# The differential attention of a two-part network on one core: projections dealt over a head's four steps, PSUM banks assigned by use, and one maximum over both score halves

## The chip, the cores and the metric

The kernel runs on one core of a Trainium2 chip. The metric is the device time of one execution in microseconds (us), median of the runs. An execution taken with the hardware profiler gives the trace. The engines are PE (TensorE, the matrix engine), DVE (VectorE), ACT (ScalarE), POOL (GpSimd) and SP (SyncE, which issues the DMA transfers).

## The reference

A first block (two layers: FFN, mixer, FFN) and a second block (two layers of another kind) run one after the other on 512 tokens of width 1024. The change lies in the mixer of the first layer, a differential attention with 8 heads, 512 queries (tokens x) and 768 keys (256 of a context y and the 512 tokens):

```python
def diff_attn_core(q, k, v, lam):
    s = jnp.einsum('bqhcd,bkhcd->bhcqk', q.astype(jnp.float32), k.astype(jnp.float32))
    p = jax.nn.softmax(s * (1.0 / math.sqrt(HEAD_DIM)), axis=-1)
    a = p[:, :, 0] - lam * p[:, :, 1]
    return jnp.einsum('bhqk,bkhe->bqhe', a.astype(v.dtype), v)
```

Each head has two halves c of 64 dimensions. q and k are normalised per half (RMS), q and the token part of k are rotated (RoPE), and v has 128 dimensions. The head's output is normalised (RMS over 128), and `w_o` maps all heads back to 1024. `lam` is a scalar from four learned vectors. Everything is float32.

## The kernel before

**Arithmetic.** Each float32 operand of a large product is split into a high part (fp32r) and the low remainder, and a product is three matmuls: high x high, high x low, low x high. ACT casts the high part (`ACT.Copy` into an R tensor), DVE subtracts to get the low part. Weights come from HBM in blocks of eight 128x128 tiles, in the order of use; ACT (L845) and DVE (L1319) split each block, four split blocks are held, and a block may be split once PE has released the one four before it (`stream(upto[...])` on ACT and DVE stands in their programs at the place where that is done).

**Order.** Five engine programs are written out by hand; each engine works its list in order, and every step waits on named steps of others. Layout is features on partitions, tokens along the free axis.

**Attention.** Head h is worked in four steps qt of 128 queries; n = 4h + qt counts to 32. In step n PE writes the scores of both halves (`scores`, 128 x 768 each, K = 64: half 0 on rows 0 to 63 of the array, half 1 on rows 64 to 127). DVE takes the maximum of each half (L1560) and scales it (L1563), ACT takes the two exponentials with row sums (L1012), and DVE combines both halves into one matrix (L1532 to L1538, `combine`). In step n+1 PE transposes that matrix (`turn`, "pt", L394), ACT (L985) and DVE (L1515) split it, and every second step PE multiplies the values with it (`values`, 18 matmuls of 256 columns). Between these stands the preparation of the next head H = h + 1, which `piece` deals out: q is projected in step 0 (24 matmuls of 512 columns), its sums of squares and its rotation (a permutation matmul) come in step 1 together with the projection of k (8 x 3 x (512 + 256) columns), the rotation of k, the projection of v and the spread of k's scales in step 2, and the transposition of v in step 3. Head h - 1's output is normalised in step 2. In the last head the output projections `wo` of heads 0 to 5 take the place of the preparation, two tiles per step, and the parts of heads 6 and 7 follow at the end.

**PSUM.** Banks 0 to 5 form a ring: `take` gives the next one or two, whatever the use, and waits until the last user has freed them. The head's output (PG, bank 6) and the sums (PN, bank 7) have banks of their own.

```python
        def take(name, n):
            nonlocal pos
            n = 2 if n > 512 else 1
            pos += -pos % n
            i = pos % 6
            pos += n
```

**lam.** It is computed by DVE at the start of attention, with an exponential of ACT (whose table load, L994, takes place there).

## Time and profile before

| what | value |
|---|---|
| runs | 3828.03, 3831.35, 3834.58 us; median 3831.35 |
| profiled execution | 3833.75 us, its span 3832.0 us, mean granted PE clock 0.948 of full |
| PE busy | 3579.2 us (93% of the span) |
| DVE, ACT, POOL busy | 1932.7, 1272.9, 350.1 us |
| chain that ended last | PE 85%, DVE 9%, ACT 3%, POOL 1% |
| attention with the norms before and after (649.7 to 1215.0 us) | 565.3 us, PE busy 488.5, DVE 306.2, ACT 210.3, clock 0.84 |

The granted clock has two levels, 2.4 GHz (1.0) and 1.2 GHz (0.5); the clock of a stretch is the mean over it. Times in rows are from the start of the span. A matmul's record is longer than its distance to the next one, since they are pipelined; distances of starts tell what one costs in a run of them. "[1.63 <-DVE QKV L1510]" behind a row is idle time of that engine before it and what ended it.

### The profile page before, as it was taken

What the parts mean: (1) busy time and instruction counts of PE and PEld (TensorE: products, weight loads), DVE (VectorE), ACT (ScalarE), POOL (GpSimd) and SP (SyncE); (2) the same over time, 40 slices, a digit from 0 to 9 for tenths busy, and PEclk for the clock granted to TensorE, in tenths of its full rate; (3) what the DMA queues carried; (4) which work ended last, traced back from release to release, by engine and by line L of the source; (5) the groups of instructions that cost most, each with busy time, mean ns of one, the idle gap of its engine ahead of it and who ended that gap; (6) DMA issues with size and microseconds to landing.
All of it is one profiled execution on the core that took longest, in us unless ns stands there. A gap on an engine that the chain in (4) does not pass through costs nothing.

```text
span 3832.0 us, 40505 instructions
## 1 busy us (share of the span) xinstructions
PE 3579.2 (93%) x17064; PEld 2949.4 (77%) x17064; DVE 1932.7 (50%) x2742; ACT 1272.9 (33%) x1771; POOL 350.1 (9%) x200
## 2 busy tenths in 40 slices
PE   2999998899998999899999999989999999999998
PEld 2888887677776888788877888766788877678887
DVE  8434334455555544454444333386564647656464
ACT  4322123333333322322333323333442433344242
POOL 3301001000101000000000000330100023010001
PEclk9999998888888999999999999998899999899999
DMA  5323232000002545354322222220122222012221
GB/s 194 135 84 127 89 116 72 33 28 28 28 34 91 185 147 170 118 173 154 116 77 81 96 99 94 85 79 6 51 98 99 95 77 84 6 50 88 99 94 60
DMA packets 95654, 348.83 MB, mean 91 GB/s; under 512 B 10608, under 2 KB 10864, under 8 KB 94960
## 3 DMA queue, kind: packets, MB, share of 16 engines
q1 hardware_dynamic: 94176, 343.06, 26.2%
q10 hardware_dynamic: 1296, 3.18, 0.2%
q8 instruction: 134, 2.20, 0.2%
q14 instruction: 48, 0.39, 0.0%
HBM read 344.10 MB, written 2.10 MB: 90 GB/s over the span
## 4 chain that ended last, share of the span: by engine, by line
PE 85%; DVE 9%; ACT 3%; POOL 1%; issue 1%; DMA 0%; ACTq 0%; SPq 0%; DVEq 0%; POOLq 0%
PE PS L325 84%; DVE CAC L1689 2%; DVE WL L1319 1%; PE PS L394 1%; DVE ST L1560 1%; ACT WH L845 1%; DVE SCR L1346 1%; POOL SM L1974 1%; ACT G L1012 0%; DVE X L1661 0%; ACT HH L896 0%; DVE ST L1780 0%; ACT G L884 0%; DVE X L1670 0%; POOL PTF L1967 0%
## 5 line engine op out<-in xcount | busy, mean ns | idle before, releaser
L325 PE MATMUL PS<-HH,WH 128*128 128x512 f32 (+1 forms) x3120 | 1204.5, 386 | 58.3 <-DVE HL L1676 18.1
L1319 DVE TENSOR_TENSOR WL<-RAW,WH 128x1024 fp32r<-128x1024 f32 x462 | 576.7, 1249 | 1261.5 <-ACT WH L845 1261.4
L325 PE MATMUL PS<-HL,WH 128*128 128x512 f32 (+1 forms) x3120 | 1187.8, 381 | 0.0
L325 PE MATMUL PS<-HH,WL 128*128 128x512 f32 (+1 forms) x3120 | 1183.1, 379 | 0.0
L845 ACT ACTIVATE WH<-RAW 128x1024 fp32r<-128x1024 f32 x496 | 524.4, 1057 | 1472.7 <-PE PS L325 1460.4
L325 PEld LDWEIGHTS PS<-HH,WH 128*128 128x128 f32 x3120 | 603.0, 193 | 183.7 <-DVE HL L1421 19.4
L325 PEld LDWEIGHTS PS<-HL,WH 128*128 128x128 f32 x3120 | 602.5, 193 | 113.7 <-issue 7.0
L325 PEld LDWEIGHTS PS<-HH,WL 128*128 128x128 f32 x3120 | 599.8, 192 | 111.1
L325 PE MATMUL PS<-AH,WH 128*128 128x512 f32 x1392 | 525.2, 377 | 0.0
L325 PE MATMUL PS<-AL,WH 128*128 128x512 f32 x1392 | 524.8, 377 | 0.0
L325 PE MATMUL PS<-AH,WL 128*128 128x512 f32 x1392 | 523.5, 376 | 0.0
L325 PEld LDWEIGHTS PS<-AH,WH 128*128 128x128 f32 x1392 | 262.5, 189 | 49.0 <-issue 0.3
L325 PEld LDWEIGHTS PS<-AH,WL 128*128 128x128 f32 x1392 | 261.8, 188 | 48.5
L325 PEld LDWEIGHTS PS<-AL,WH 128*128 128x128 f32 x1392 | 262.3, 188 | 47.6
L1346 DVE CUSTOM_DVE_ANT_0 RAW<-RAW,PTF 128x1024 f32<-128x1024 f32 x128 | 154.0, 1236 | 26.4 <-POOL PTF L1967 26.4
L2010 POOL TENSOR_TENSOR ACC<-ACC,X 128x512 f32<-128x512 f32 x25 | 32.3, 1292 | 1270.6 <-DVE X L1908 692.0
L1987 POOL TENSOR_TENSOR ACC<-ACC,G 128x512 f32<-128x512 f32 (+1 forms) x30 | 42.8, 1428 | 1131.7 <-ACT G L869 831.0
L919 ACT ACTIVATE AH<-G 128x512 fp32r<-128x512 f32 (+1 forms) x88 | 60.4, 686 | 210.1 <-DVE G L1435 210.1
L1974 POOL TENSOR_TENSOR SM<-SM,MH 128x4 f32<-128x4 f32 (+3 forms) x42 | 70.1, 1671 | 595.4 <-DVE SM L1379 595.2
L1689 DVE SCALAR_TENSOR_TENSOR CAC<-CIN,VB,CAC 128x512 f32<-128x512 f32 x120 | 109.2, 955 | 0.9
L1438 DVE TENSOR_TENSOR AL<-G,AH 128x512 fp32r<-128x512 f32 (+1 forms) x88 | 69.4, 789 | 66.2 <-ACT AH L919 66.2
L1967 POOL TENSOR_TENSOR PTF<-RAW,PTF 128x1024 f32<-128x1024 f32 x28 | 79.3, 2830 | 220.8 <-ACT PTF L853 116.1
(266 smaller groups left out, 3321.5 us busy)
## 6 DMA issues: line engine op xcount, KB each, us to landing
RAW<-wst SPq DMA_DIRECT2D x640, 512.0 KB, 3.3
X<-xT SPq DMA_DIRECT2D x1, 2048.0 KB, 12.3
out<-X SPq DMA_DIRECT2D x8, 256.0 KB, 2.0
PTF<-cb SPq DMA_DIRECT2D x1, 1024.0 KB, 4.9
Y<-yT SPq DMA_DIRECT2D x1, 1024.0 KB, 6.3
PTF<-cb ACTq DMA_DIRECT2D x1, 1024.0 KB, 4.8
HM<-sg ACTq DMA_DIRECT2D x4, 256.0 KB, 3.6
ROPE<-rope SPq DMA_DIRECT2D x1, 512.0 KB, 4.2
```

Of the source, the lines that this page charges most:

```text
L325: return e.matmul(o, l, r, start=start, stop=stop)
L394: m = e.transpose(bk[:, t * 128:(t + 1) * 128], src[:, t * 128:(t + 1) * 128], ident)
L845: e.activation(split_block(b)[0], raw_block(s), ACT.Copy).then_inc(*did("act_done", ("whi", b)))
L919: e.activation(aview(f - f0, N)[0], s, ACT.Copy).then_inc(*did("act_done", ("ahi", st, f)))
L1319: e.tensor_tensor(lo, raw_block(s), f32(hi), ALU.subtract).then_inc(*did("dve_done", ("wlo", b)))
L1346: e.tensor_tensor_reduce(dst, raw, CB[:, 0:1024], 1.0, 0.0, ALU.mult, ALU.add, mcol(l, ch, k, 0)).then_inc(*did("dve_done", ("gx", l, j)))
L1438: e.tensor_tensor(lo, s, f32(hi), ALU.subtract).then_inc(*did("dve_done", ("a", st, f), ("gdone", use)))
L1560: e.tensor_reduce(s8[:, c:c + 1], bank["s", n, c][:, 0:768], AXX, ALU.max).then_inc(*did("dve_done", ("max", n, c)))
L1689: e.scalar_tensor_tensor(out=CA[i], in0=AP[i][:, k:k + 512], scalar=v2(f"caw{l}", i * 31 + k), in1=CA[i], op0=ALU.mult, op1=ALU.add).then_ ...
L1967: e.tensor_tensor((PROD, SCR[3])[p], raw_block(s), CB[:, 1024:2048], ALU.mult).then_inc(*did("pool_done", ("gprod", l, j)))
L1974: e.tensor_tensor(sm(name, b, n), sm(name, a, n), MH[:, 0:n], ALU.pow).then_inc(*did("pool_done", ("rs", name)))
L1987: e.tensor_tensor(ACC[:, 0:N], ACC[:, 0:N], G(use, N), ALU.add).then_inc(*did("pool_done", ("acc", up, m), ("gdone", use)))
```

## The change

Nothing is computed otherwise; order, buffers and banks change, only in the attention and in the place of `lam`.

- **Projections over all four steps.** Step 0: k of head H (with the transposition of head h's v between its halves, in `between`). Step 1: sums of k's squares, q (k's permutation in the middle). Step 2: sums of q's squares, the last 256 columns of v ("v2", q's permutation in the middle), the spread of k's scales, the sums for head h - 1's output. Step 3: the spread for that output, the first 512 columns of v. ACT evicts each at the start of the next step, ahead of the softmax. k and q no longer share scratch buffers (KS_, KSQ, QS, QSQ, `vs(h)`).
- **PSUM by use** (`hold`). Banks 0 to 2: scores. 3 and 4: transposed probabilities, transposed v, spread of k. 5 (and 6 for k): projections. 6: sums, permutations, spread of o. 7: head outputs. The other stages still use `take`.
- **Scores.** Both halves lie in 1536 contiguous columns of three banks. The matmuls alternate between the halves; a wait of PE on its own "s bank 1" keeps the two halves from writing bank 1 at once. One reduction takes both maxima and one operation scales both; both exponentials wait for it, and both halves are freed by the second.
- **Last head and tail.** `wo` tiles 2, 2, 2, 1 per step and one after the last transposition, all in bank 5; then six tiles together for heads 6 and 7, head 7's sums and spread between their first and second K tile, two more tiles singly.
- **Start.** Head 0 is projected k, q, v2, v one after another, and k of head 1 before the first scores.
- **lam** is worked out before the first norm, from a small tensor with a DMA of its own.

PE's program, cut to its core (`key_stat` and `key_permute` have sisters for q, `key_spread`, `out_stat` and `out_spread` for the rest, of the same form):

```diff
+        def hold(name, n, i, frees=None):
+            n = 2 if n > 512 else 1
+            prior = [u for u in users[i:i + n] if u is not None]
+            users[i:i + n] = [frees or ("free", name)] * n
+            bank[name] = PS[:, i * 512:(i + n) * 512]
+            return bank[name], prior
...
             i = pos % 6
             pos += n
-            prior = [u for u in users[i:i + n] if u is not None]
-            users[i:i + n] = [name] * n
-            bank[name] = PS[:, i * 512:(i + n) * 512]
-            return bank[name], prior
+            return hold(name, 512 * n, i)
         def allowed():
             nonlocal ptr
...
+            def project(name, us, c0, c1, into, final=True, between=None):
+                nonlocal released
+                bk, prior = hold(name, c1 - c0, into)
+                q.wait_ge("wlo", us[0][2])
+                for p in prior:
+                    q.wait_ge(*p)
+                for k, (hi, lo, step, _) in enumerate(xs):
+                    q.wait_ge(*step)
+                    if k == 4 and between:
+                        between()
+                    for c in range(c0, c1, 512):
+                        d = min(c + 512, c1)
+                        o = bk[:, c - c0:d - c0]
+                        mm(o, us[k][0], hi[:, c:d], k == 0, False)
+                        mm(o, us[k][0], lo[:, c:d], False, False)
+                        m = mm(o, us[k][1], hi[:, c:d], False, k == 7)
+                steps = [("tile", name)]
+                if final:
+                    steps.append(("wfree", us[0][2]))
+                    released += 1
+                m.then_inc(*did("pe_done", *steps))
+                upto[name] = allowed()
...
+            def key_stat(h):
+                stat(("k", h), [(KSQ, 128, bd, ("ksq", h))], 6, 2, into=6)
+            def key_permute(h):
+                permute(("pk", h), permA, KS_[:, 0:512], ("ks", h), into=6)
...
+            def turn_values(h):
+                bk, prior = hold(("vt", h), 768, 3)
+                a, b = vs(h)
+                for p in prior:
+                    q.wait_ge(*p)
+                q.wait_ge("vs", h)
+                for t in range(4):
+                    e.transpose(bk[:, t * 128:(t + 1) * 128], a[:, t * 128:(t + 1) * 128], ident)
+                q.wait_ge("vs2", h)
+                for t in range(2):
+                    m = e.transpose(bk[:, 512 + t * 128:640 + t * 128], b[:, t * 128:(t + 1) * 128], ident)
+                m.then_inc(*did("pe_done", ("tile", ("vt", h))))
...
             def scores(n):
                 h, qt = n // 4, n % 4
-                for c in range(2):
-                    bk, prior = take(("s", n, c), NT)
-                    rows = slice(c * 64, c * 64 + 64)
...
+                _, prior = hold(("s", n), 768, 0)
+                _, more = hold(("s", n), 512, 2)
+                o = bank["s", n] = PS[:, 0:1536]
+                q.wait_ge("qsplit", h)
+                q.wait_ge("ksplit", h)
+                for p in prior + more:
+                    q.wait_ge(*p)
+                Q = [[a[c * 64:c * 64 + 64, qt * 128:qt * 128 + 128] for a in QKV[h % 2]] for c in range(2)]
+                K = [[a[c * 64:c * 64 + 64, 512:1280] for a in QKV[h % 2]] for c in range(2)]
+                for i, (a, b) in enumerate(((0, 0), (0, 1), (1, 0))):
+                    m = mm(o[:, 512:768], Q[0][a], K[0][b][:, 512:768], i == 0, i == 2)
+                    if i == 2:
+                        m.then_inc(*did("pe_done", ("s bank 1", n)))
+                    mm(o[:, 1024:1536], Q[1][a], K[1][b][:, 256:768], i == 0, i == 2)
+                for i, (a, b) in enumerate(((0, 0), (0, 1), (1, 0))):
+                    m = mm(o[:, 0:512], Q[0][a], K[0][b][:, 0:512], i == 0, i == 2)
+                    if i == 2:
+                        m.then_inc(*did("pe_done", ("s first", n)))
+                    q.wait_ge("s bank 1", n)
+                    m = mm(o[:, 768:1024], Q[1][a], K[1][b][:, 0:256], i == 0, i == 2)
+                m.then_inc(*did("pe_done", ("tile", ("s", n))))
...
+            project(("k", 0), weights(1024, 0), 0, NT, 5)
+            project(("q", 0), weights(0, 0), 0, NX, 0)
+            key_stat(0)
+            v = weights(2048, 0)
+            project(("v2", 0), v, NX, NT, 3, False, lambda: key_permute(0))
+            project(("v", 0), v, 0, NX, 4)
+            query_stat(0)
+            query_permute(0, 0)
+            key_spread(0, 1)
             for n in range(32):
-                h, qt = n // 4, n % 4
+                h, qt, H = n // 4, n % 4, n // 4 + 1
+                if n == 0:
+                    project(("k", 1), weights(1024, 1), 0, NT, 5, True, lambda: turn_values(0))
                 scores(n)
-                if qt == 2 and h:
-                    stat(("o", h - 1), [(OSQ, 128, ones, ("osq", h - 1))], 4, 1)
                 if n >= 3 and n % 2:
                     values((n - 2) // 4, (n - 2) % 4 // 2)
                 if n:
-                    turn(("pt", n - 1), G(("p", n - 1, 0)), 6, ("pc", n - 1), ("gdone", ("p", n - 1, 0)))
-                if h < 7:
-                    piece(h + 1, qt)
+                    turn_p(n - 1)
+                if H < 8:
+                    if qt == 0 and n:
+                        project(("k", H), weights(1024, H), 0, NT, 5, True, lambda: turn_values(h))
+                    if qt == 1:
+                        key_stat(H)
+                        project(("q", H), weights(0, H), 0, NX, 5, True, lambda: key_permute(H))
+                    if qt == 2:
+                        query_stat(H)
+                        v = weights(2048, H)
+                        project(("v2", H), v, NX, NT, 5, False, lambda: query_permute(H, 6))
+                        key_spread(H, 3)
+                        if h:
+                            out_stat(h - 1)
+                        if H == 7:
+                            project(("v", H), v, 0, NX, 5)
+                    if qt == 3:
+                        if h:
+                            out_spread(h - 1)
+                        if H < 7:
+                            project(("v", H), v, 0, NX, 5)
                 else:
-                    for m in (2 * qt, 2 * qt + 1):
-                        lin([output(m, 0, 6)], oxs(0, 6))
-                if qt == 2 and h:
-                    spread(("o", h - 1), 4, None, ("rs", ("o", h - 1)))
-            turn(("pt", 31), G(("p", 31, 0)), 6, ("pc", 31), ("gdone", ("p", 31, 0)))
+                    if qt == 0:
+                        turn_values(7)
+                    if qt == 2:
...
+                    for m in ((0, 1), (2, 3), (4, 5), (6,))[qt]:
+                        lin([output(m, 0, 6)], oxs(0, 6), [5])
+                        if m == 4:
+                            out_spread(6)
+            turn_p(31)
...
+            lin([output(7, 0, 6)], oxs(0, 6), [5])
             values(7, 1)
-            stat(("o", 7), [(OSQ, 128, ones, ("osq", 7))], 4, 1)
-            spread(("o", 7), 4, None, ("rs", ("o", 7)), ("attention done",))
-            lin([output(m, 6, 8) for m in range(4)], oxs(6, 8))
-            for m in range(4, 8):
-                lin([output(m, 6, 8)], oxs(6, 8))
+            def last():
+                out_stat(7)
+                out_spread(7, ("attention done",))
+            lin([output(m, 6, 8) for m in range(6)], oxs(6, 8), [0, 1, 2, 3, 4, 5], {1: last})
+            for m in (6, 7):
+                lin([output(m, 6, 8)], oxs(6, 8), [m - 6])
```

ACT's program, in part:

```diff
+            def softmax(n):
+                h, qt = n // 4, n % 4
+                s8 = st8(n)
+                for c in range(2):
+                    use = ("p", n, c)
+                    q.wait_ge("gdone", GBEFORE[use])
+                    q.wait_ge("negmax", n)
+                    steps = [("exp", n, c)]
+                    if c:
...
-                h, qt = n // 4, n % 4
-                for c in range(2):
-                    s8, use = st8(n), ("p", n, c)
-                    q.wait_ge("gdone", GBEFORE[use])
-                    q.wait_ge("negmax", n, c)
-                    steps = [("exp", n, c), ("free", ("s", n, c))]
-                    if qt == 3 and c == 1:
-                        steps.append(("smfree", ("q", h)))
-                    e.activation(G(use), bank["s", n, c][:, 0:768], ACT.Exp, bias=s8[:, 2 + c:3 + c],
-                                 scale=sm(("q", h), 24 + qt * 2 + c, 1), accum_out=s8[:, 4 + c:5 + c]).then_inc(*did("act_done", *steps))
+                h, qt, H = n // 4, n % 4, n // 4 + 1
+                if qt == 0 and n:
+                    v_evict(h)
+                if H < 8:
+                    if qt == 1:
+                        k_evict(H)
+                    if qt == 2:
+                        q_evict(H)
+                    if qt == 3:
```

DVE's and SP's programs, in part:

```diff
-            e.tensor_tensor(LMS[:, 64:128], lamv[:, 128:192], lamv[:, 192:256], ALU.mult).then_inc(*did("dve_done", ("lam1",)))
+            q.wait_ge("lam in")
+            e.tensor_tensor(LMS[:, 0:64], LAMV[:, 0:64], LAMV[:, 64:128], ALU.mult).then_inc(*did("dve_done", ("lam0",)))
...
+            def row_max(n):
+                s8, r = st8(n), sm(("q", n // 4), 24 + n % 4 * 2, 2)
+                q.wait_ge("tile", ("s", n))
+                e.tensor_reduce(s8[:, 0:2], bank["s", n].rearrange("p (c k) -> p c k", c=2), AXX, ALU.max).then_inc(*did("dve_done", ("max", n)))
+                q.wait_ge("max", n)
+                q.wait_ge("qscale", n // 4)
+                e.scalar_tensor_tensor(out=s8[:, 2:4], in0=s8[:, 0:2], scalar=-1.0, in1=r, op0=ALU.mult, op1=ALU.mult).then_inc(*did("dve_done", ("negmax", n)))
...
-                    stat(("o", h - 1), 1, 4, 1.0 / 128, 1e-6)
+                h, qt, H = n // 4, n % 4, n // 4 + 1
+                row_max(n)
+                if H < 8 and qt == 1:
+                    stat(("k", H), 1, 12, 1.0 / 64, 1e-6)
+                if H < 8 and qt == 2:
+                    stat(("q", H), 1, 8, 1.0 / 64, 1e-6)
                 if n:
                     p_split(n - 1)
                 combine(n)
-                if h < 7:
-                    if qt == 0 and h:
-                        stream(upto["q", h + 1])
+                if H < 8:
+                    if qt == 0 and n:
+                        v_split(h)
+                        stream(upto["v", h])
                     if qt == 1:
-                        q_rotate(h + 1)
-                        stream(upto["k", h + 1])
+                        k_rotate(H)
+                        stream(upto["k", H])
                     if qt == 2:
-                        k_rotate(h + 1)
-                        stream(upto["v", h + 1])
...
+                e.dma_start(LAMV[:, :], vec1[:, V1["lam"][0]:NV1]).then_inc(*did("lam_in", ("lam in",), by=16))
```

## Rows read from the trace of the kernel before

**Rows 1.** The page: the chain that ended last, by engine.
```profile
PE 85%; DVE 9%; ACT 3%; POOL 1%; issue 1%; DMA 0%; ACTq 0%; SPq 0%; DVEq 0%; POOLq 0%
```
**Rows 2.** Windows: us, busy (count) of PE, PEld, DVE, ACT, POOL; clock, DMA share, GB/s.
```profile
656.60:720.40 63.80, 45.02 (x187) 36.25 (x187) 25.33 (x41) 25.51 (x36) 4.28 (x2) 0.76 0.10 34
720.40:768.10 47.70, 43.44 (x232) 35.53 (x233) 28.14 (x50) 17.24 (x27) 4.67 (x2) 0.84 0.07 22
...
1112.90:1198.40 85.50, 73.85 (x344) 61.13 (x344) 44.10 (x67) 25.52 (x39) 4.61 (x4) 0.83 0.15 50
768.10:1112.90 344.80, 317.95 (x1721) 261.67 (x1720) 197.58 (x336) 129.94 (x204) 34.01 (x18) 0.88 0.08 28
```
**Rows 3.** Waits of PE, 649 to 1225 us: total, times, longest.
```profile
PE PS L325 <- ACT G L1012: 10.1, 15, 2.4
```
**Rows 4.** Timeline of DVE in one step of the steady part.
```profile
883.08 0.95 DVE L1560 TENSOR_REDUCE ST<-PS 128x1 f32<-128x768 f32 x1
...
885.18 0.21 DVE L1563 TENSOR_SCALAR ST<-ST,SM 128x1 f32<-128x1 f32 x1
887.24 0.96 DVE L1515 TENSOR_TENSOR PTL<-PS,PTH 128x768 fp32r<-128x768 f32 x1 [1.85 <-ACT PTH L985]
...
889.15 1.02 DVE L1538 SCALAR_TENSOR_TENSOR G<-G,ST 128x768 f32<-128x768 f32 x1
```
**Rows 5.** Timeline of ACT in the same step.
```profile
884.31 0.99 ACT L1012 ACTIVATE G<-PS,ST,SM 128x768 f32<-128x768 f32 x1 [4.28 <-DVE ST L1563]
...
886.41 0.80 ACT L985 ACTIVATE PTH<-PS 128x768 fp32r<-128x768 f32 x1
```
**Rows 6.** Timeline of PE: end of k's projection, scores, sums, transposition.
```profile
906.52 0.40 PE L325 MATMUL PS<-HH,WH 128*128 128x512 f32 x1
...
907.22 0.28 PE L325 MATMUL PS<-HH,WH 128*128 128x256 f32 x1
907.34 0.28 PE L325 MATMUL PS<-HL,WH 128*128 128x256 f32 x1
...
907.66 0.62 PE L325 MATMUL PS<-QKV 64*128 64x512 f32 x2
908.13 0.39 PE L325 MATMUL PS<-QKV,QKV 64*128 64x512 f32 x1
...
909.37 1.05 PE L325 MATMUL PS<-CST,Y 128*128 128x1 f32 x8
910.43 0.87 PE L394 MATMUL PS<-CST,G 128*128 128x128 f32 x6
```
**Rows 7.** Timeline of PE, a permutation.
```profile
898.24 1.10 PE L325 MATMUL PS<-Y,CST 128*128 128x512 f32 x2
```
**Rows 8.** Groups of DVE and POOL, 720 to 1170 us: count, busy, mean ns, idle.
```profile
L1319 DVE TENSOR_TENSOR WL<-RAW,WH 128x1024 fp32r<-128x1024 f32 x25 | 30.6, 1225 | 93.0 <-ACT WH L845 92.9
...
L1386 DVE TENSOR_TENSOR Y<-PS,ROPE 128x512 f32<-128x512 f32 x14 | 9.6, 682 | 0.0
...
L1974 POOL TENSOR_TENSOR SM<-SM,MH 128x4 f32<-128x4 f32 x7 | 7.0, 1006 | 96.9 <-DVE SM L1379 96.9
```
**Rows 9.** Timeline of PE behind the gap at a head's last step.
```profile
883.31 1.51 PE L394 MATMUL PS<-CST,G 128*128 128x128 f32 x6 [1.63 <-DVE QKV L1510]
```
**Rows 10.** Windows: the same place, columns as in rows 2.
```profile
882.20:889.00 6.80, 5.07 (x14) 3.98 (x15) 4.81 (x10) 2.87 (x5) 0.00 (x0) 0.50 0.00 0
```
**Rows 11.** Timeline of PE in the tail: output projection of heads 6, 7.
```profile
1185.33 0.80 PE L325 MATMUL PS<-HH,WH 128*128 128x512 f32 x1 [1.45 <-DVE HL L1527]
```
**Rows 12.** Timeline of DVE in the start of attention: last normed tile, lam.
```profile
670.07 0.96 DVE L1421 TENSOR_TENSOR HL<-G,HH 128x768 fp32r<-128x768 f32 x1 [1.12 <-ACT HH L896]
...
690.73 0.22 DVE L1465 TENSOR_TENSOR LMS<-VA 128x64 f32<-128x64 f32 x1
...
691.33 0.14 DVE L1469 TENSOR_SCALAR SGV<-VA 128x1 f32<-128x1 f32 x1
```
**Rows 13.** Timeline of PE: the first scores.
```profile
720.36 0.58 PE L325 MATMUL PS<-QKV 64*128 64x512 f32 x2 [2.50 <-DVE QKV L1510]
```

More of the change, by code:

```diff
@@ L1364, in stat @@
         def stat(name, nsrc, n, inv, eps):
-            sums = PN[:, 0:n]
+            region = bank["st", name]
+            sums = region[:, 0:n]
             q.wait_ge("stat", name)
@@ L1919, in _ @@
         stream(upto["start"])
+        lam()
         norm("f00")
```

346 lines of the change are left out of this document (175 added, 171 removed).

## Prediction

> **What bounds the kernel now.** I read the page first: PE carries 85% of the chain that ended last [rows 1], so time is won only where PE works, waits, or runs at the low clock. Then windows by stage: the change touches the 541.8 us from 656.6 to 1198.4. In it lie the start up to the first scores (63.8 us), head 0 (47.7), the stretch from head 0's end to head 7 (344.8, six heads, 57.5 each) and head 7 with the tail (85.5) [rows 2]. In the six heads the clock means 0.88: with the two levels 2.4 and 1.2 GHz that is 24% of the time, 13.8 us a head, at 1.2 GHz.
>
> Next, what PE's work costs at 2.4 GHz, by distances of starts: three matmuls of 512 columns take 907.22 - 906.52 = 0.70 us, one of 256 0.12 us, so a K tile of 768 columns takes 1.05, k's or v's projection 8.3 and q's 5.6 us. A set of scores takes 909.37 - 907.66 = 1.71 us, a transposition 0.87, sums 0.13 per matmul (1.05 for eight) [rows 6], a permutation 1.1 [rows 7]. Values are 18 x 0.12 = 2.2 us a pair. One head: projections 22.2, scores 6.8, values 4.4, transpositions 5 x 0.7 = 3.5 (they overlap their neighbours a little), 28 sums and 20 spread matmuls 6, permutations 2.2, together 45. The other 12.5 us of a head are idle and low clock. Waits that the list names are small, the largest 10.1 us for exponentials in all of attention [rows 3], and the gap at a head's last step, where no projection lies, is 1.6 us before a transposition that then runs at half speed (1.51 us, against 0.87) [rows 6, 9]; the 6.8 us from 882.2 on all lie at 1.2 GHz [rows 10]. So what is to be had is the idle time, and more than it the low clock behind it.
>
> **The change, part by part.** The count of projections, values, transpositions and sums stays.
>
> Scores: the rows of before already show the two halves overlapping. Twelve matmuls in sequence would be 6 x 0.23 + 6 x 0.12 = 2.1 us, and they took 1.71 [rows 6]. Alternated, each half needs 1.05, and the wait on bank 1 sits in the middle; the bounds are 1.05 and 2.1, and I take 1.4, nearer to 1.05 than 1.71 is, with one restart in it. That saves 0.3 a step. The Trainium skill (TensorEngine Tiling (Array Packing), Theoretical Speedup) gives up to twofold for a contraction of 64; by it 2.1 would become 1.05 and 32 sets would save 21 us rather than my 10 against 1.71. The overlap in the row agrees with it in part.
>
> Maximum: two reductions of 768 at 0.95 and two scalings of 0.21 took 885.39 - 883.08 = 2.31 us [rows 4]. One over 1536: bounds 0.95 (if columns were free) and 1.9. Operations of 512 took 0.68 [rows 8] and of 768 0.96 [rows 4], 0.28 for 256 columns; so 0.95 + 0.8 = 1.75, plus one scaling 0.21: 1.96. But the first exponential no longer starts beside the second maximum. From the end of the scaling, two exponentials take 886.41 - 884.31 = 2.1 [rows 5], the high part 0.8, then DVE 0.96 to the split and 2.0 more to the combined matrix [rows 4]: split at +3.95, combined at +6.0. Per step DVE's chain is 8.0 us where it was 7.1 (885.39 - 883.08, then 1.85 idle, then 890.17 - 887.24).
>
> Steady head: the loop that closes. I count from the end of step 2's scaling. Combined +6.0; q's rotation (three of 0.68) and scale 2.1; split of a weight block 1.23; k_scale 0.96; k_split 0.84 on ACT and 0.96; with the small ones DVE is free at +12.4 [rows 4, 8]. Step 3: maximum 1.96, +14.35; combined +20.35, q_split +21.05. Only then may PE begin the next head's scores (they wait for "qsplit"). Step 0: scores 1.4 and 0.15 until DVE sees them, maximum 1.96: +24.6. Bank 3 is free when the probabilities before are split, +28.5; the transposition of v 0.7 and k's second half 4.15 follow: +33.4. Step 1: scores 1.4, values 2.2, transposition 0.66, sums 1.4, q 5.6 and permutation 1.1: +45.7. Step 2: 1.55 and 1.96: +49.2. So 49.2 us a head at 2.4 GHz, of which PE works 45 - 1.2 = 44. The other 5.2 are idle: in step 0 before v's transposition (about 1.3), in step 2 before the spread (0.7) and before head h - 1's sums (2.1; they share bank 6 with q's permutation, which DVE frees only after combining), and the rest, 1.1, at the end of step 3, where the maximum waits for DVE and not for PE.
>
> What is gained is that DVE and ACT no longer stand behind the projection of their own step, since each eviction comes a step later; what is added are these bank waits. Queued behind a waiting PE are all its later matmuls; DVE's maximum and the exponentials wait for the next scores.
>
> Low clock: step 2's stretch of waits, spread and sums looks like the stretch at 883 [rows 9, 10]. I expect one fall a head, 6.8 us as there, costing PE 3.4, of which the slack in step 3 takes some: +2.3, with bounds 0 and the 6.9 of before. For restarts behind waits I add 0.5. Sum 52, against 57.5: 6 x 5.5 = 33 us.
>
> Start: k of head 0 goes along with the norm, whose last tile ends at 671.0 [rows 12], and is done at about 673. Then q 5.6, sums 1.4, v in two parts 8.3, permutation 1.1, sums 1.05, permutation 1.1, spread 1.4, k of head 1 8.3 and v's transposition 0.7: 29 us, and 1.5 for low clock: first scores at 703.5 in place of 720.36 [rows 13]. Head 0 then lacks that k and transposition: 49.2 - 7 = 42.3 and 2.5 for clock, 45, against 47.7. Together 16.9 + 2.7 = 19.5.
>
> Head 7 and tail, from the first maximum: `wo` tiles of 18 matmuls, 4.15 each, share one bank, so each second one of a step waits for DVE's addition (0.9). Steps end (next scaling) at 19.4, 33.9 and 48.6; combined 54.6, tile 7 59.7, values 62, six tiles' first K part 66, in whose wake sums, POOL's power (1.0 [rows 8]), spread, scale and split end at 71.7; second part 76, two more tiles 78.7. With 3.5 for clock 82.2; before it was 85.5 less the 1.4 of the scores ahead of that maximum, 84.1: 2 won [rows 2]. What the six tiles hide is the wait between the last values and 1185.3, 1.45 us idle before it [rows 11]; the single bank gives part of it back.
>
> lam: four small operations, 691.47 - 690.73 = 0.74 us [rows 12], leave attention's start (in the 16.9 already) and stand before the first norm, where DVE goes from its streaming straight to the sums: +0.7, not hidden. The extra DMA is one issue on SP, weighed at nothing: it stands where SP's next blocks wait for buffers, and uncovered it would delay the first norm by the time of one issue.
>
> Sum: 33 + 19.5 + 2 - 0.7 = 54 us. The profiled execution took 3833.75, 1.75 outside its span; 3833.75 - 54 = 3779.8, and the median of the runs lies 2.4 lower: 3777.
>
> **Rivals.**
> *A, forecast (0.50):* 3777, own range 3757 to 3795.
> *B, the clock stays up (0.17).* The even spread of projections leaves no stretch sparse enough. For it: the spans with a projection run at 1.0. Against it: step 2. Without 6 x 2.3, head 0's 2.5, the start's 1.5, the tail's 3.5 and the restarts' 3: 54 + 24 = 78, 3753.
> *C, the longer DVE chain and the clock eat it (0.19).* 8.0 in place of 7.1 per step, and a fall behind each of three gaps, so that a head loses 6.9 as before: 6 x 4.6 = 28 less, 26 gained: 3805. The Trainium skill (TensorEngine Tiling (Array Packing), PSUM Bottleneck) says tiling speeds up TensorE, not the evacuation of PSUM; by it the maximum and exponentials stay the bound whatever the scores take. The step chain above, with 6 us of DVE and ACT behind 1.4 of scores, bears that out.
> *D, slower (0.10).* Alternating the halves breaks the pipelining: the pair at the head of a set took 0.47 us and not 0.35 (907.66 to 908.13) [rows 6]. If each matmul ran its own 0.40 or 0.28, a set would cost 6 x 0.40 + 6 x 0.28 = 4.1, 2.7 above mine. Three of four sets lie on the loop, and of the fourth the slack of step 3 covers about half: 28 x 2.7 = 76 us, and the change ends 22 us above before, 3853. It decides from a set of 1.4 + 54/28 = 3.3 us on.
> *E, no change (0.04).* Bank 5 or 6 waits on evictions that come a step late and moves the same idle time: 3831. Against it: ACT's evictions stand ahead of the softmax and cost two operations of some 0.8 [rows 5] where the scores and the maximum take 3.5.
>
> **Chances and range.** About 0.2% (8 us) is what a measurement of this kernel tells from no change. Faster: A, B, C and 0.01 of D (sets just under 3.3), 0.87; within 0.2% 0.04; slower 0.09. The range takes B below and C above, with the bounds of scores (1.05 and 2.1: 18 x 0.35 = 6 less, 18 x 0.7 = 13 more) partly: 3745 to 3812.
>
> **What would show it.** First scores near 703; distances of the first maxima of heads near 52 us; a set of scores at 1.2 to 1.5; one reduction of 1.75; PE idle before the spread and sums of step 2 and before a head's first scores; clock above 0.88 in the six heads. Wrong if sets take over 2 us, if PE waits for weight blocks, or if a bank's release stands behind something in DVE's or ACT's list that I placed too early.

## The result, and the profile after

The kernel went from 3830.98 us (median of 4 runs, 3828.03 to 3834.58) to 3772.03 us (4 runs, 3770.19 to 3780.0): ratio 0.985, 95% interval 0.9833 to 0.9867, 59 us faster. The forecast was 3777, from a sum of 54. The profiled execution of the changed kernel has a span of 3769.1 us, and the chain that ended last still lies with PE (the same line of the page as in [rows 1]; the fences below have the columns of the groups of rows before):

```profile
PE 85%; DVE 9%; ACT 3%; POOL 1%; issue 1%; DMA 0%; SPq 0%; ACTq 0%; DVEq 0%; POOLq 0%
```

Windows by stage, to be laid beside [rows 2]: start, head 0, heads 1 to 5, head 6, head 7 with the tail.

```profile
656.50:700.20 43.70, 39.86 (x210) 33.21 (x210) 23.48 (x36) 23.39 (x34) 3.90 (x2) 0.96 0.08 25
700.20:746.70 46.50, 38.06 (x206) 29.83 (x206) 27.13 (x43) 17.05 (x29) 4.17 (x2) 0.84 0.11 34
746.70:989.70 243.00, 229.99 (x1431) 192.10 (x1432) 153.57 (x235) 103.83 (x170) 24.55 (x15) 0.95 0.10 33
989.70:1049.00 59.30, 48.59 (x292) 39.72 (x292) 34.37 (x54) 23.87 (x40) 4.91 (x3) 0.91 0.08 27
1049.00:1139.60 90.60, 71.52 (x344) 57.23 (x344) 42.63 (x60) 27.36 (x41) 3.78 (x4) 0.87 0.18 59
```

Stage by stage in both traces; a head goes from the start of its first maximum to that of the next head:

| stage | before | after | difference |
|---|---|---|---|
| first projection to first scores | 63.8 | 43.8 | -20.0 |
| head 0 | 47.9 | 44.8 | -3.1 |
| heads 1 to 5, together | 284.1 | 243.0 | -41.1 |
| head 6 | 60.6 | 59.2 | -1.4 |
| head 7, tail to the last `wo` matmul | 84.1 | 90.7 | +6.6 |
| from there to `f01`'s first matmul | 16.6 | 17.5 | +0.9 |
| all that follows | 2617.0 | 2612.0 | -5.0 |

So the gain is in two places: the start, and five of the six steady heads. Four of these take 48.3 us each (steps of 12.4, 12.2, 13.4 and 10.3) and the fifth 49.8, where they took 56 to 57.5. Head 6 won 1.4 us and the tail lost 6.6. The last line of the table lies far behind the change. In the traces of the twelve experiments, which have no edit there, the same stretch took from 2611.3 to 2617.8 us, so a difference of 5 us in it is nothing of the change.

PE in one steady head: the wait of step 0, a set of scores with the values behind it, then the two waits of step 2.

```profile
849.17 0.66 PE L504 MATMUL PS<-CST,ACC 128*128 128x128 f32 x4 [0.87 <-DVE PTL L1632]
...
854.16 0.50 PE L336 MATMUL PS<-QKV 64*128 64x256 f32 x2
...
855.63 0.39 PE L336 MATMUL PS<-PTH,QKV 128*128 128x256 f32 x1
...
873.77 1.61 PE L336 MATMUL PS<-CST,Y 128*128 128x128 f32 x12 [0.46 <-DVE PTL L1632]
876.83 1.05 PE L336 MATMUL PS<-CST,OSQ 128*128 128x1 f32 x8 [1.45 <-DVE Y L1504]
```

A set takes 855.63 - 854.16 = 1.47 us from start to start, 1.71 before [rows 6]. The three waits are the ones that the prediction placed (bank 3 twice, bank 6 once), smaller than it had them (0.87, 0.46 and 1.45 for 1.3, 0.7 and 2.1). DVE's groups, stretch 700 to 1140 us (columns as in rows 8), show one maximum of 1.76 and one scaling of 0.16:

```profile
L1649 DVE TENSOR_REDUCE ST<-PS 128x2 f32<-128x1536 f32 x32 | 56.2, 1756 | 45.1 <-PE PS L336 45.1
L1652 DVE SCALAR_TENSOR_TENSOR ST<-ST,SM 128x2 f32<-128x2 f32 x32 | 5.1, 161 | 1.1
```

The low clock is down to one stretch a head. In heads 1 to 4 it lasts 3.4 us and begins with step 3's scores (first window below); in head 5 it lasts 6.8 us (second window), and this is the head that took 49.8. Below them stand a whole head of the first kind, at 0.96, and head 5, at 0.93 (0.88 in [rows 2]).

```profile
878.20:881.60 3.40, 3.40 (x19) 2.68 (x17) 2.56 (x5) 1.11 (x2) 1.01 (x1) 0.53 0.46 154
973.80:980.60 6.80, 6.80 (x34) 5.99 (x35) 5.21 (x8) 1.80 (x3) 1.01 (x1) 0.51 0.20 77
...
843.38:891.66 48.28, 45.51 (x287) 37.89 (x287) 30.71 (x48) 20.77 (x34) 4.91 (x3) 0.96 0.10 33
939.96:989.72 49.76, 46.99 (x287) 39.33 (x287) 30.73 (x48) 20.76 (x34) 4.91 (x3) 0.93 0.09 33
```

In the two places that disappoint, the timeline of PE names the waits: in head 6 v's second part behind its own first part's eviction, and the next head's first scores behind q's split; in the tail the second tile of a step behind DVE's addition (bank 5), and in the middle of step 2 the spread for head 6's output behind POOL, which works out its scale.

```profile
1027.11 0.79 PE L336 MATMUL PS<-HH,WH 128*128 128x512 f32 x1 [2.89 <-ACT Y L1057]
...
1044.89 0.50 PE L336 MATMUL PS<-QKV 64*128 64x256 f32 x2 [4.42 <-DVE QKV L1601]
...
1078.08 0.50 PE L336 MATMUL PS<-HH,WH 128*128 128x512 f32 x1 [2.40 <-DVE X L1668]
...
1094.24 1.01 PE L336 MATMUL PS<-CST,SM 128*128 128x128 f32 x3 [4.28 <-POOL SM L2118]
```

### The profile page after: what moved, and what is told of

Read it like the earlier page. It is cut to its first block, busy times and chain, and to the rows that moved or that the text cites. A ratio compares the mean times of both kernels' runs of the same rounds, so it can differ in the third digit from the quotient of the medians.

```text
span 3769.1 us, 40441 instructions
## 1 busy us (share of the span) xinstructions
PE 3522.2 (93%) x17064; PEld 2902.4 (77%) x17064; DVE 1918.5 (51%) x2678; ACT 1269.6 (34%) x1779; POOL 343.6 (9%) x200
## 4 chain that ended last, share of the span: by engine, by line
PE 85%; DVE 9%; ACT 3%; POOL 1%; issue 1%; DMA 0%; SPq 0%; ACTq 0%; DVEq 0%; POOLq 0%
PE PS L336 84%; DVE CAC L1832 2%; ACT G L1101 1%; PE PS L408 1%; DVE ST L1649 1%; DVE SCR L1463 1%; DVE WL L1436 1%; POOL SM L2118 1%; DVE X L1804 0%; DVE PTL L1632 0%; ACT HH L984 0%; ACT G L972 0%; ACT WH L933 0%; DVE ST L1923 0%; ACT PTH L1082 0%
## 5 line engine op out<-in xcount | busy, mean ns | idle before, releaser
L336 PEld LDWEIGHTS PS<-AH,WH 128*128 128x128 f32 x1392 | 262.4, 189 | 49.1 <-issue 0.3
L336 PEld LDWEIGHTS PS<-AH,WL 128*128 128x128 f32 x1392 | 261.8, 188 | 48.8
L2154 POOL TENSOR_TENSOR ACC<-ACC,X 128x512 f32<-128x512 f32 x25 | 32.3, 1291 | 1268.1 <-DVE X L2051 691.2
## 6 DMA issues: line engine op xcount, KB each, us to landing
X<-xT SPq DMA_DIRECT2D x1, 2048.0 KB, 12.2
```

What stands on the lines that cost most here:

```text
L336: return e.matmul(o, l, r, start=start, stop=stop)
```

## The experiments

Ratios are to the kernel before, which was run beside each; its own median went from 3830.4 to 3832.0 us between these groups of runs, so two kernels whose medians lie 2 us apart are not told apart by them. "Head" is the distance of first maxima in heads 1 to 5 of the one profiled execution; "49.8 once" means one of the five.

| kernel | median us | ratio, 95% | head, us |
|---|---|---|---|
| changed | 3772.0 | 0.985 (0.9833 to 0.9867) | 48.3, 49.8 once |
| v in step 2 | 3830.9 | 0.9999 (0.999 to 1.0008) | 57.3 to 58.1 |
| v of head 7 in step 3 | 3762.7 | 0.9822 (0.9809 to 0.9836) | 47.8, 48.3 once |
| scores in turn | 3773.7 | 0.9852 (0.9839 to 0.9866) | 48.8, 50.3 once |
| two maxima | 3779.1 | 0.9862 (0.9849 to 0.9875) | 48.8 to 49.1, 50.2 once |
| cast in own step | 3776.1 | 0.9858 (0.9843 to 0.9873) | 48.4 to 49.9 |
| tail, two banks | 3765.4 | 0.9828 (0.9813 to 0.9842) | 48.3, 47.8 once |
| start together | 3783.4 | 0.9875 (0.9859 to 0.9892) | 48.3, 49.8 once |
| DVE chain short | 3757.5 | 0.9806 (0.9792 to 0.9821) | 46.8 to 49.8 |
| sums in bank 7 | 3761.1 | 0.9818 (0.9805 to 0.9831) | 47.9 |
| all of these | 3731.9 | 0.9743 (0.973 to 0.9757) | 45.3 |
| all, and the gaps | 3725.9 | 0.9729 (0.9715 to 0.9742) | 44.3, 44.5 once |
| the last, scores in turn | 3727.6 | 0.9734 (0.972 to 0.9747) | 44.6, 44.8 once |

**The dealing undone (v in step 2).**

```diff
-                        if H == 7:
-                            project(("v", H), v, 0, NX, 5)
+                        project(("v", H), v, 0, NX, 5)
...
-                        if H < 7:
-                            project(("v", H), v, 0, NX, 5)
```

> One part of the change undone: v's last 512 columns are projected in step 2, right behind its first part and the spread, for every head, and step 3 has no projection. Theory (most of the 41 us that heads 1 to 5 gained, 57 to 48.3 us each, comes from having a projection in every step): step 3 becomes a gap again, a head takes 53 to 57 us, the kernel ends 35 to 55 us above the changed one, near 3810 to 3825. Rival (the gain comes from the scores, the one maximum and the banks dealt by use): a head stays under 50 us and the kernel within 12 us of the changed one.

Measured: 3830.87, and a ratio of 0.9999 to the kernel before. All 59 us go, though scores, maximum, banks and start stay. That the two times meet is chance: the start keeps its 20 us, heads 1 to 5 take 289.6 us, 46.6 more than in the changed kernel and 5.4 more than before, head 0 takes 52.7 and the tail 90.9. One head in windows, and PE's two new waits in it:

```profile
872.00:930.07 58.07, 48.84 (x287) 40.28 (x288) 30.81 (x48) 20.66 (x34) 4.91 (x3) 0.88 0.08 28
```

```profile
909.36 0.80 PE L336 MATMUL PS<-HH,WH 128*128 128x512 f32 x1 [2.89 <-ACT Y L1054]
...
927.49 0.80 PE L336 MATMUL PS<-QKV 64*128 64x256 f32 x2 [4.42 <-DVE QKV L1598]
```

These are head 6's two waits, to the hundredth. In all 58.07 - 48.28 = 9.8 us a head: 2.89 + 4.42 of new waits less the 0.87 of step 0, which is gone, and 3.3 by which PE is busy longer for the same matmuls (48.84 for 45.51), at a clock of 0.88 instead of 0.96. Theory held, beyond its upper end. One reservation: 2.89 of it is bank 5, which v's first part still holds; that is the price of this dealing in these banks, not of any dealing. No run has v in step 2 with a bank of its own.

**Head 6 (v of head 7 in step 3).**

```diff
-                        if H == 7:
-                            project(("v", H), v, 0, NX, 5)
...
-                        if H < 7:
-                            project(("v", H), v, 0, NX, 5)
+                        project(("v", H), v, 0, NX, 5)
...
+                if n == 28:
+                    for i in range(6):
+                        o_split(i)
...
-                    if n == 27:
-                        for i in range(6):
-                            o_split(i)
```

> The one head that did not profit: head 6 took 59.2 us where heads 1 to 5 took 48.3, and in it v of head 7 is projected in step 2. Here v of head 7 is projected in step 3 like all others, and the splits of the six finished heads' outputs, which must follow it, move from the end of step 27 to the start of step 28 (ScalarE) and behind step 28's high part (VectorE). Theory (the place of v is the cause): head 6 falls to 48 to 50 us, some 2 us come back in step 28, the kernel ends 7 to 10 us below the changed one. Rival (the six splits are the cause, wherever they stand): they move their cost to head 7, and the kernel stays within 3 us.

Measured: 9 us below the changed kernel, as the theory had it; head 6 takes 47.84 us instead of 59.2 (maxima below), and head 7 with the tail takes 1.7 more, with the six splits in step 28. That the sum fits so well is in part luck: in the trace head 6 won 11.4 us and heads 1 to 5, which have no edit, 3.5 (the next paragraph says by what), while the stretch behind attention took 5.7 more than in the changed kernel's trace.

```profile
986.24 1.76 DVE L1646 TENSOR_REDUCE ST<-PS 128x2 f32<-128x1536 f32 x1 [1.06 <-PE PS L336]
...
1034.08 1.76 DVE L1646 TENSOR_REDUCE ST<-PS 128x2 f32<-128x1536 f32 x1 [1.06 <-PE PS L336]
```

Its steady heads tell more. They keep the 1.45 us wait and yet heads 2 to 6 run at full clock throughout, for a gain of only half a microsecond each; in place of the low clock PE now waits for q's split:

```profile
842.77:890.60 47.83, 44.19 (x287) 36.70 (x287) 30.72 (x48) 20.77 (x34) 4.92 (x3) 1.00 0.11 34
```

```profile
888.99 0.50 PE L336 MATMUL PS<-QKV 64*128 64x256 f32 x2 [0.86 <-DVE QKV L1598]
```

So in the changed kernel a head is not PE's: the loop through DVE and ACT sets it at about 47.8, and the short fall of the clock lay in PE's slack. The changed kernel's own head says the same. In the run with two banks in the tail, whose edit begins only in head 7, head 5 had no fall and took 47.82; with the fall of 3.4 us the head takes 48.3, with one of 6.8 us 49.8. A short fall costs 0.5, and one twice as long 2.0.

```profile
939.99:987.81 47.82, 44.19 (x287) 36.71 (x287) 30.70 (x47) 20.74 (x34) 4.91 (x3) 1.00 0.10 34
```

**Scores in turn.** Same banks, same maximum; the six matmuls of rows 0 to 63 first, then the six of rows 64 to 127.

```diff
-                    mm(o[:, 1024:1536], Q[1][a], K[1][b][:, 256:768], i == 0, i == 2)
+                for i, (a, b) in enumerate(((0, 0), (0, 1), (1, 0))):
+                    m = mm(o[:, 0:512], Q[0][a], K[0][b][:, 0:512], i == 0, i == 2)
+                for i, (a, b) in enumerate(((0, 0), (0, 1), (1, 0))):
+                    mm(o[:, 1024:1536], Q[1][a], K[1][b][:, 256:768], i == 0, i == 2)
```

> The scores of the two halves are no longer alternated: the six matmuls of rows 0 to 63 first, then the six of rows 64 to 127, in the same three banks and behind the same single maximum. Theory (alternating is worth what a set shows, 1.42 us against 1.71 before): a set takes 1.7 to 2.1 us, and with three of four sets on the loop the kernel ends 6 to 16 us above the changed one. Rival (the sets lie beside VectorE's work or the clock gives it back): less than 3 us. If sequence were the faster order, a set would be under 1.4 us and the kernel faster.

Measured: 1.7 us above, inside the intervals. A set takes 854.77 - 853.17 = 1.60, so alternating is worth 0.13 us a set, and not the 0.3 and more that was expected:

```profile
853.17 0.38 PE L336 MATMUL PS<-QKV 64*128 64x256 f32 x1
...
854.77 0.39 PE L336 MATMUL PS<-PTH,QKV 128*128 128x256 f32 x1
```

By the kernel's time the rival held. The heads say something else: with a fall of 3.4 us in both traces a head takes 48.79 for 48.30, and that is four sets of 0.13. So the sets are not hidden; they are short. The kernel shows less than the heads do because head 0 took 2.1 us less in this execution, with 6.8 us at the low clock behind its first scores where the changed kernel's had 13.7. Alternating is worth some 3 us of the 59 in the six steady heads. What the new banks add to it (1.71 a set before, 1.60 here) was not taken apart.

**Two maxima.**

```diff
-                e.tensor_reduce(s8[:, 0:2], bank["s", n].rearrange("p (c k) -> p c k", c=2), AXX, ALU.max)
+                for c in range(2):
+                    e.tensor_reduce(s8[:, c:c + 1], bank["s", n][:, c * 768:(c + 1) * 768], AXX, ALU.max)
```

(with a scaling behind each). 

> The one maximum over both halves becomes two reductions of 768 columns with a scaling each, and both exponentials wait for the second (as they read the middle bank that the second reads too). Theory (VectorE's chain of maximum, exponentials, combination is on the loop in three of four steps): the reductions take 2.3 us where they took 1.92, and 24 to 28 steps of 0.4 us cost 8 to 12 us. Rival (PE sets the pace in the steady heads, VectorE has room): less than 3 us.

Measured: 7 us above in the median, a head 0.5 longer in the trace and PE's waits of step 0 and 2 longer (1.13 for 0.87, 0.72 for 0.46). The four runs lie between 3770.3 and 3782.7 and the intervals overlap, so the size is uncertain; six heads of 0.5 are 3 us. The direction agrees with the theory, and the price of 0.4 on four steps arrives by a third. That both exponentials must wait for the second maximum is a matter of the middle bank, in which both halves lie. The Trainium skill (PSUM — Partial Sum Buffer, PSUM bank collisions raise a hardware error) counts two engines reading one bank at once as a collision; no run here tried it.

**Cast in own step.** `stream(upto["k", H])` and its like stand at the end of the step of their projection, on ACT and DVE.

> Each weight block that a projection releases is cast and split at the end of that projection's own step, as in the kernel before, instead of one step later; all else stays as changed. Theory (what the dealing gains is in part that ScalarE and VectorE no longer stand behind the projection of their own step): the cast of 1.06 us and the split of 1.22 then begin when the projection ends, and the next maximum, whose scores are done 1.4 us after that end, starts about 0.9 us late in steps 1, 2 and 3: 2 to 3 us a head, 12 to 20 us in all. Rival (the spread of the projections alone does it, the place of the casts is free): within 4 us of the changed kernel.

Measured: 4 us above, with intervals that overlap. Steps became 13.2, 12.2, 12.2 and 10.8 or 12.3: step 0 lost 0.8 and step 2 won 1.2. The heads without a fall of the clock take 48.45, where such a head takes 47.82 with the casts one step later, so this place costs 0.6 us a head and not the expected 2 to 3. The heads with a fall take 49.9.

**Tail, two banks.**

```diff
-                        lin([output(m, 0, 6)], oxs(0, 6), [5])
-                        if m == 4:
-                            out_spread(6)
+                        lin([output(m, 0, 6)], oxs(0, 6), [5 + m % 2])
+                        if m == 5:
+                            out_spread(6, into=5)
```

> Head 7 and the tail took 90.7 us where I had 82.2. Here the output tiles of head 7 alternate between banks 5 and 6, and the spread for head 6's output stands behind tile 5 and not behind tile 4, in bank 5. Theory (the single bank and the wait of 4.28 us for POOL's power ahead of that spread make the difference): PE's idle time in the tail falls by 6 to 8 us and the kernel ends 5 to 8 us below the changed one. Rival (the three steps of head 7 are set by VectorE's chain, and PE waits somewhere else instead): within 2 us.

Measured: 6.7 us below. Head 7 and the tail take 82.5 us instead of 90.7, which is what I had forecast for the changed kernel (82.2). The edit is two in one, a second bank and a later spread, and no run has one without the other; the lists below show the waits for DVE's addition down by 2.4 us and those for POOL by 4.3. PE's waits in that stretch, changed kernel first, then this one:

```profile
PE PS L504 <- DVE PTL L1632: 6.4, 1, 6.4
PE PS L336 <- POOL SM L2118: 5.6, 2, 4.3
PE PS L336 <- DVE X L1668: 4.9, 4, 2.4
```

```profile
PE PS L504 <- DVE PTL L1632: 6.1, 1, 6.1
PE PS L336 <- DVE X L1668: 2.5, 3, 0.9
...
PE PS L336 <- POOL SM L2118: 1.3, 1, 1.3
```

**Start together.** The three projections of head 0 interleaved by K tile, sums and permutations behind them. 

> Head 0's three projections are interleaved by K tile again, as before the change, so that all three end together, and the sums and permutations of keys and queries follow both; the rest is as changed. Theory (of the 20 us that the start gained most comes from k's and q's evictions lying beside v's projection): the first scores come 6 to 12 us later, as sums, permutations and the keys' rotation have only head 1's k projection ahead of the spread, and the kernel ends 5 to 12 us above the changed one. Rival (interleaved, PE is denser beside the norm, which delivers its last tile 14 us after the first matmul, and earns that back): within 2 us or faster.

Measured: 11 us above; the first scores come at 708.73 instead of 700.24, 8.5 us later, and the heads are those of the changed kernel. So the order of projections, sums and permutations, with the banks that it needs, is 8.5 of the start's 20 us. Most of it lies ahead of the first projection, which waits for all its banks at once and starts at 664.39 instead of 656.46; later the queries' sums wait for the keys' rotation:

```profile
664.39 0.77 PE L336 MATMUL PS<-HH,WH 128*128 128x512 f32 x1 [13.62 <-DVE G L1558]
...
694.16 1.87 PE L336 MATMUL PS<-CST,Y 128*128 128x2 f32 x8 [1.46 <-DVE Y L1529]
```

The other 11.6 us can be placed by the traces. In this run head 0's projections end where they end before the change (their last matmul starts at 688.17, there at 688.02), and from there to the first scores it takes 20.6 us, before 32.3. PE's waits in this stretch are 2.7 us here and 13.6 before, the first of them behind ACT's queue with lam's table load in it (1.28 us, at 689.58):

```profile
692.76 1.87 PE L325 MATMUL PS<-CST,Y 128*128 128x2 f32 x8 [4.36 <-ACT Y L938]
```

How much of this is lam's new place and how much the new order of ACT's evictions, no run separates.

**DVE chain short.** On top of the late v: casts, splits of weight blocks and q's split move ahead, into the time in which ACT waits for the maximum and DVE for the exponentials.

```diff
                 row_max(n)
+                if H < 8 and qt == 0 and n:
+                    stream(upto["v", h])
...
+                if H < 8 and qt == 3:
+                    q_split(H)
```

> On top of e2_v7_in_step3: the cast and split of a weight block and the split of q move from the end of a step into the 2.3 to 2.8 us in which ScalarE waits for the maximum and VectorE for the exponentials. Nothing else changes. Theory (a steady head is set by the chain of VectorE and ScalarE from step 2's scores to the next head's first scores, 1.22 us of split in step 2 and 0.7 us of q's split on it; PE's idle 0.86, 0.46 and 1.45 us are its mark): a head falls from 47.8 to 45.5 to 46.5, the kernel ends 9 to 14 us below e2_v7_in_step3. Rival (PE sets the head, its clock falls as soon as idle time moves): less than 3 us, with the low clock back. A second rival (VectorE's split taken early delays the split of the probabilities): slower by up to 5 us.

Measured: 5 us below the kernel that it starts from, between theory and rival. That median stands for no execution: the four runs lie in two pairs, 3753.1 and 3753.2, 3761.8 and 3761.9, that is 10 us and 1 us below. The trace is from the upper pair. In it head 1 took 46.8 at full clock as PE's work and waits make it; in the others the low clock was back, and they took 48.3 with 3.4 us of it and 49.8 with 6.8. Here a fall costs its whole price, 1.5 or 3.0 us, where the longer chain of DVE hid all but 0.5 of the short one; so rival and theory are both right in part. That the lower pair had fewer falls is a guess; there is no trace of it. The wait for q's split is gone, and the two of step 2 are not (first a head with the short fall, then head 1):

```profile
888.12:936.38 48.26, 45.49 (x287) 37.92 (x287) 30.69 (x47) 20.77 (x35) 5.82 (x3) 0.96 0.11 33
743.22:790.03 46.81, 44.19 (x287) 36.82 (x288) 30.69 (x48) 20.71 (x34) 5.82 (x3) 1.00 0.10 35
```

```profile
918.52 1.60 PE L336 MATMUL PS<-CST,Y 128*128 128x128 f32 x12 [0.46 <-DVE PTL L1629]
921.57 1.05 PE L336 MATMUL PS<-CST,OSQ 128*128 128x1 f32 x8 [1.45 <-DVE Y L1501]
```

**Sums in bank 7**, on the late v alone: `out_stat(h - 1, 7)`, and DVE reads it ahead of `k_scale`. 

> On top of e2_v7_in_step3 alone: the sums of head h - 1's output go to bank 7, which is free from the squares of that output to the next values, instead of bank 6 behind q's permutation. It removes the idle 1.45 us ahead of them. Theory (in e2_v7_in_step3 VectorE's chain sets a head, in e8_dve_chain_short PE does): here the idle time only moves, to the wait for q's split before the next head's first scores (0.86 to about 2.3 us), a head stays at 47.5 to 48.3, the kernel within 3 us of e2_v7_in_step3. Rival (PE sets the head here too): 6 x 1.4 = 8 us faster.

Measured: 1.7 us below its base, intervals overlapping, head 47.9. The 1.45 us are gone and 1.21 stand in front of the values instead, as they need bank 7 from DVE: the wait moved, as DVE's chain holds the head, but to another place than I had written. Each of these heads has a fall of 3.4 us and is still at 47.9.

```profile
877.59 0.58 PE L336 MATMUL PS<-PTH,QKV 128*128 128x256 f32 x1 [1.21 <-DVE SM L1494]
```

**All of these.** 

> Everything that helped together: v of head 7 in step 3, the shorter VectorE chain, the sums of the output in bank 7, and the output tiles in two banks. Theory (with the chain shortened PE sets the head: 46.8 us at full clock in the one head of e8_dve_chain_short without a fall, of which 1.45 is the wait for bank 6): a head falls to 45.3 to 46.5 and the low clock of 3.4 us a head, which began behind that wait, goes; 5 to 7 heads x 2 to 3 us = 12 to 18, and 6 us in the tail as in e6_tail_two_banks: 18 to 24 us below e8_dve_chain_short, 3733 to 3740. Rival (the clock falls elsewhere, behind the next shortest wait): a head stays at 48, and only the tail's 6 us are won, 3751.

Measured: 3731.88, a little below the expected 3733 to 3740. Every head from 1 to 6 takes 45.30 us at full clock. The bank that was worth at most 1.7 us while DVE held the head is worth about 19 on the shortened chain (3757.5 - 3731.9 = 25.6, less the tail's 6.7; heads 1 to 6 in the two traces: 291.2 and 271.8). The wait of 1.45 us is half of that, six times; the other half is the low clock, which was in five of these six heads and is in none now.

**All, and the gaps.** The spread behind the sums of the output, v's transposition after five K tiles of k. 

> e10_all with the two waits for bank 3 moved behind work that is ready: v's transposition one K tile later (five instead of four K tiles of k ahead of it), and the spread of the keys' roots behind the sums of the output. Theory (PE sets the head, so idle time is time): 0.87 + 0.46 us less idle a head, 1.3 x 7 = 9 us below e10_all if the heads are at full clock there. Rival (the splits of v and k come later, VectorE's chain sets the head again): within 3 us.

Measured: 3725.86, 6 us below and not 9, with heads of 44.27: the two waits of 0.87 and 0.46 are gone, but 0.67 us stand in front of the values instead. It is the fastest kernel here, 105 us below before. The windows of one head in the last two:

```profile
833.66:878.96 45.30, 43.90 (x287) 36.61 (x287) 30.71 (x48) 20.77 (x35) 5.83 (x3) 1.00 0.11 35
```

```profile
832.70:876.97 44.27, 43.60 (x287) 36.62 (x287) 30.72 (x48) 20.76 (x35) 5.82 (x3) 1.00 0.11 36
```

**The same edit where PE holds the head.** 

> The edit of e3_scores_in_turn, which there lengthened a set of scores from 1.42 to 1.67 us and cost the kernel only 1.7 us, made on e11_all_gaps. Theory (there VectorE's chain set the head and hid PE's longer sets; in e11_all_gaps PE sets it, with 0.67 us idle a head): four sets a head cost 0.25 us each, a head goes from 44.27 to 44.6 to 45.3, the kernel 4 to 8 us above e11_all_gaps. Rival (a set's length is hidden here too): a head stays within 0.2 and the kernel within 2 us.

Measured: 3727.59, 1.7 us above, intervals overlapping; a head 44.55, 0.28 longer. By the kernel the rival held, by the head neither: four sets of 0.13 are 0.5, and PE's last wait took 0.2 of them (0.67 to 0.48). My 0.25 a set was wrong: what counts is the distance to the start of what follows, 1.60 less 1.47. The premise was wrong as well: on the chain that DVE sets the sets cost a head 0.5, and here, where PE sets it, 0.28.

## Why the prediction was right, and where it was not

The places of the gain, the loop that sets a head and the waits inside it were as predicted. The length of the low clock, head 6 and the tail were not, and these errors offset each other.

*What bounds a head.* "The loop that closes" was counted at 49.2 us; at full clock it takes 47.8 (late v), and it runs where I had put it, through DVE from step 2's scores to q's split. The 1.4 us too much lie in this part: q's split ends 19.6 us behind step 2's scaling, counted at 21.05, each combination at 5.6 instead of 6.0. Shortening that chain moved the bound to PE, whose 44 us of work I had counted: the last kernel's heads take 44.27.

*Low clock.* This term was too large. I added 2.3 us a head for one fall of 6.8 and 0.5 for restarts. The price of such a fall was right: the one head that had it took 2.0 more than 47.8. Its length was not: in the other four heads it lasts 3.4 us and costs 0.5, since PE has slack in this loop. The restarts show nowhere. With 5 x 52 = 260 forecast and 243.0 measured it is 17 us more gain, 7 from the shorter loop, 7.5 from the clock and 2.5 from the restarts.

*Start.* First scores at 700.24, not 703.5; the clock stands at 0.96 from the first projection to the first scores (0.76 before), and PE's only waits there are five of some 0.75 us for the normed tiles. Head 0: 44.8 against 45.

*Head 6.* The step that took it as one of six like heads failed. v of head 7 stands in step 2 in the diff, and so step 3 has no projection: 59.2 for 52, 7 us.

*Tail.* "2 won" were 6.6 lost. The single bank was priced at 0.9 per second tile; the waits were up to 2.4. POOL's 4.28 ahead of the spread for head 6 was in no term of the sum. Steps 1 and 2 of head 7 took 16.8 and 18.4 us where I had 14.5 and 14.7. The run with two banks and the later spread took most of these waits away and landed at my figure.

*Scores and maximum.* Sizes as predicted (1.47 start to start for 1.4; 1.76 and 0.16 for 1.75 and 0.21), their worth not: alternating is worth 0.13 us a set against the same banks in turn, 0.5 us a head. The reason against rival D holds with room, 1.47 against its point of 3.3.

*lam.* In the trace the first norm comes 0.83 us late, and by 150 us that is gone, and so it is 0 in place of 0.7.

*Rivals.* The time lies in A's own range, on B's side, and for B's reason in part: the clock rose to 0.95 in heads 1 to 5, though it did not stay up. C had the right loop (DVE's chain does set the head) and the wrong price. The rule that stood with it, that tiling speeds TensorE and not the emptying of PSUM (the Trainium skill, TensorEngine Tiling (Array Packing), PSUM Bottleneck), agrees with the 1.7 us that the kernel lost with the scores in turn; the heads agree less, as each paid the full 0.5 us of its four longer sets.

In the sum the errors offset: 17 us too little in the heads, 3 in the start, 1 with lam and head 0, and 5 in the stretch behind attention, against 7 too much in head 6, 9 in the tail and 1 behind it: 54 + 26 - 17 = 63, the difference of the two spans. The medians differ by 59. The total was closer than its terms, and that is luck.

## What to carry to other kernels

Deal work so that every step has something for PE while the others finish, and look at the one step that is dealt differently: it cost 9 us here. When two chains are nearly equal (47.8 for DVE, 46.8 for PE), a fix to either alone shows little, and both together show more than their sum; before setting a fix aside, ask which wait comes up in its place. One more PSUM bank for a row of tiles, with a spread moved one tile later, was worth 7 us. And compare stages as well as medians: here a stretch without any edit differed by over 6 us between traces, and one shorter fall of the clock hid what longer scores cost.

## What the hardware showed

The same wait pattern, 0.46 and 1.45 us of idle PE behind v's first part, went with a fall of the granted clock in each head of the changed kernel and with none in the steady heads of the late v; with the late v and the sums in bank 7, where the 1.45 us are gone, every head had one of 3.4 us again. It is not the program alone that decides: head 5 of the changed kernel, unedited in the run with two banks in the tail, had 6.8 us of low clock in one execution and none in the other. What decides stays open.

What a fall costs depends on who sets the head. With DVE's chain in front a head took 47.8 without a fall, 48.3 with 3.4 us and 49.8 with 6.8 us of low clock; with the shortened chain it took 46.8, 48.3 and 49.8.

Two halves of scores on different rows of the array overlap even in turn: twelve matmuls, 2.1 us at their own distances [rows 6], took 1.71 in turn in the ring of banks, 1.60 in turn in the three new banks and 1.47 alternated, all far from the 1.05 of full overlap.
